# Fewer key chunks, a turned-query chunk for four heads, and the attention's first scores placed before the last value chunk

## The reference

```
proj = h @ w_in;  qa, ka, va, c_q, c_kv, k_r = split(proj)
q = (rmsnorm(c_q) @ w_uq).reshape(b, s, 8, 64 + 32)
q_nope, q_rope = q[..., :64], rope(q[..., 64:], cos, sin)
kv = (rmsnorm(c_kv) @ w_ukv).reshape(b, s, 8, 64 + 64)
k_nope, v = kv[..., :64], kv[..., 64:];  k_rope = rope(k_r, cos, sin)
sc = (q_nope . k_nope + q_rope . k_rope) * (64 + 32) ** -0.5
p = softmax(sc);  o = p @ v
```

## Time and profile before

| | |
|---|---|
| median of 3 runs | 1660.78 us (1659.16 to 1661.2) |
| profiled execution, its own time | 1662.77 us |
| its span, first to last instruction | 1660.7 us |
| mean granted TensorE clock | 0.996 |
| PE, DVE, ACT busy | 1620.9, 1235.5, 888.2 us |
| weight stream read | 282.68 MB at 171 GB/s over the span |

### The profile page before, as it was taken

One profiled execution on the slowest core, in us unless ns is written; L12 is line 12 of the kernel. 1 busy time (PEld: TensorE's weight loads), 2 busy tenths in 40 slices (PEclk: granted clock), 3 DMA queues, 4 the chain that ended last, 5 costly groups with the idle time before them and its releaser, 6 DMA issues.

```text
span 1660.7 us, 28594 instructions
## 1 busy us (share of the span) xinstructions
PE 1620.9 (98%) x10584; PEld 1468.4 (88%) x10584; DVE 1235.5 (74%) x1841; ACT 888.2 (53%) x1154; POOL 42.8 (3%) x55
## 2 busy tenths in 40 slices
PE   9989999999999999999999999999999999999998
PEld 8878999978899999878999999877999997899997
DVE  5765887778787787875887777447687787878787
ACT  5475545464764556565645464544554556665453
POOL 0001000000000000000000014000000000000000
PEclk9999999999999999999999999999999999999999
DMA  7253554544365544431554545543555454255543
GB/s 284 95 180 115 204 197 171 189 165 177 130 226 188 191 177 178 152 127 52 187 199 170 190 160 207 203 152 108 189 196 201 163 191 178 107 173 185 194 177 126
DMA packets 42113, 284.65 MB, mean 171 GB/s; under 512 B 4960, under 2 KB 5088, under 8 KB 9152
## 3 DMA queue, kind: packets, MB, share of 16 engines
q1 hardware_dynamic: 39840, 274.43, 45.2%
q0 software_dynamic: 2208, 9.32, 1.6%
HBM read 282.68 MB, written 1.05 MB: 171 GB/s over the span
## 4 chain that ended last, share of the span: by engine, by line
PE 84%; DVE 9%; issue 3%; ACT 3%; DMA 1%; DVEq 0%; SPq 0%; POOL 0%; ACTq 0%
PE bank L1774 14%; PE bank L1776 14%; PE bank L1775 14%; PE bank L1868 8%; PE bank L1869 8%; PE bank L1870 8%; PE bank L1820 4%; PE bank L1821 4%; PE bank L1822 4%; DVE w_lo L992 2%; DVE arena L1271 1%; ACT w_hi L554 1%; PE bank L1756 1%; PE bank L1917 1%; PE bank L2170 1%
## 5 line engine op out<-in xcount | busy, mean ns | idle before, releaser
L1774 PE MATMUL bank<-h_hi,w_hi 128*128 128x256 f32 (+1 forms) x2240 | 642.7, 287 | 9.8 <-DVE w_lo L992 6.3
L1775 PE MATMUL bank<-h_hi,w_lo 128*128 128x256 f32 (+1 forms) x2240 | 636.7, 284 | 0.0
L1776 PE MATMUL bank<-h_lo,w_hi 128*128 128x256 f32 (+1 forms) x2240 | 636.7, 284 | 0.0
L1774 PEld LDWEIGHTS bank<-h_hi,w_hi 128*128 128x128 f32 x2240 | 429.9, 192 | 18.2 <-issue 9.5
L1775 PEld LDWEIGHTS bank<-h_hi,w_lo 128*128 128x128 f32 x2240 | 430.0, 192 | 4.5 <-issue 1.4
L1776 PEld LDWEIGHTS bank<-h_lo,w_hi 128*128 128x128 f32 x2240 | 429.9, 192 | 0.9
L992 DVE TENSOR_TENSOR w_lo<-raw,w_hi 128x2048 fp32r<-128x2048 f32 (+3 forms) x115 | 244.9, 2132 | 115.2 <-ACT w_hi L554 114.9
L1298 DVE TENSOR_TENSOR w_lo<-raw,w_hi 128x2048 fp32r<-128x2048 f32 x145 | 327.6, 2285 | 1.6 <-ACT w_hi L753 1.6
L741 ACT ACTIVATE arena<-arena,par 128x256 f32<-128x256 f32 x220 | 120.5, 595 | 357.9 <-DVE arena L1257 354.6
L753 ACT ACTIVATE w_hi<-raw 128x2048 fp32r<-128x2048 f32 x150 | 286.1, 1907 | 19.8 <-PE bank L1870 19.7
L554 ACT ACTIVATE w_hi<-raw 128x2048 fp32r<-128x2048 f32 (+2 forms) x110 | 194.3, 1772 | 106.9 <-PE bank L1870 39.0
(11 more groups left out here) (196 smaller groups left out, 1294.2 us busy)
## 6 DMA issues: line engine op xcount, KB each, us to landing
raw<-wstream SPq DMA_DIRECT2D x254, 1024.0 KB, 4.8
arena<-window_bias POOLq DMA_DIRECT2D x4, 768.0 KB, 7.9
raw<-wstream SPq DMA_DIRECT2D x8, 256.0 KB, 3.1
arena<-dilated_bias POOLq DMA_DIRECT2D x8, 256.0 KB, 3.4
arena<-conv_rows POOLq DMA_DIRECT2D x2, 1024.0 KB, 4.8
raw<-wstream SPq DMA_DIRECT2D x4, 384.0 KB, 3.5
cst<-consts SPq DMA_DIRECT2D x1, 1088.0 KB, 11.7
x<-x_in SPq DMA_DIRECT2D x2, 512.0 KB, 5.1
```

What stands on the lines that cost most here:

```text
L1774: nc.tensor.matmul(dst, w_parts[0], x_parts[0], start=start, stop=False, **kw)
L1775: nc.tensor.matmul(dst, w_parts[1], x_parts[0], start=False, stop=False, **kw)
L1776: return nc.tensor.matmul(dst, w_parts[0], x_parts[1], start=False, stop=stop, **kw)
```

## The change

The rotated 32 columns of four heads now share a tile, and their swapped halves another, so that chunks 9 and 10 are all of the turned parts, 11 and 12 the plain parts of four heads each. Keys of two heads share a tile, and a chunk has four heads: two key chunks (13, 14) in place of four, since the unused value columns are no longer in them. The value chunks become 15 and 16, w_o 17 to 20. DVE's products with the tables cover 128 partitions of 256, for four heads at once, and its sums are one for each head, 32 partitions of 256; the tables are laid out four times down the partitions. ACT copies plain queries and keys head by head, four copies of 64 x 256 for each chunk.

PE computes the scores of heads 0 and 1 after the key chunks, before the value chunks (in nat before the last two), once the banks are free. The values go to banks outside the ring of three (`value_banks`). The wait for their copies moves to the first product with the values, and ACT makes the copies after the exponentials of heads 0 and 1 and before the first transposed copy.

There are four slots for bias tables instead of two; the two new ones lie in lat, free once the latents are normalized. In the mixer, ACT's split of chunk 5 moves ahead of the first reciprocal root. In nat, the split of chunk 13 moves from ahead of the attention into it, in halves (ACT at heads 2 and 3, DVE at 4 and 5), and ACT's halves of chunk 14 from heads 3 and 5 to 5 and 6.

```diff
-        return [CH] * 9 + [2 * 3 * P] * 4 + [2 * 2 * P] * 4 + [2 * 256] * 2 + [CH] * 4
+        return [CH] * 9 + [2 * 3 * P] * 4 + [2 * 2 * P] * 2 + [2 * 256] * 2 + [CH] * 4
...
+        def value_banks(name, c):
+
+            return (bank[4], bank[5]) if name == "mix" or c == 8 else (bank[6], bank[7])
...
+        def bias_slot(h):
+
+            return bias_a[:, h % 4, :] if h % 4 < 2 else flat(lat[:, 2 * (h % 4) - 4:2 * (h % 4) - 2, :])
...
-                        if h >= 2:
-                            pool.wait_ge(biased, bias_count(h - 2))
-                        pool.dma_start(bias_a[:, h % 2, :], bias_in[:, h * 512:(h + 1) * 512]).then_inc(bias_full[h % 2], 16)
+                        if h == 2:
+                            pool.wait_ge(hlo_done, DT + 5)
+                        if h >= 4:
+                            pool.wait_ge(biased, bias_count(h - 4))
+                        pool.dma_start(bias_slot(h), bias_in[:, h * 512:(h + 1) * 512]).then_inc(bias_full[h % 4], 16)
...
+                    if n == 1:
+                        last_values()
...
-                        if c:
+                        if c not in (0, 3):
...
+                            split_hi(c0 + 5)
                             inv_sqrt()
...
-                    for c in range(9, 19):
-                        if c < 17:
-                            split_hi(c0 + c + 2)
-                        src = bank[(c0 + c) % 3]
-                        if c < 17:
-                            dst = q_b if c < 13 else k_b
-                            j = (c - 9) % 4
-                            evac(c0 + c, dst[0:64, 2 * j:2 * j + 2, :], halves(src[0:64, :]), 1.0 if c < 13 else SCALE_B)
-                        elif c == 18:
-                            value_evac(c0 + 17, v_b, scaled=False, heads=0)
+                    for c in range(9, 15):
+                        split_hi(c0 + c + 2)
+                        if c >= 11:
+                            dst, src = (q_b, k_b)[c // 13], bank[(c0 + c) % 3]
+                            act.wait_ge(chunk_used, c0 + c + 1)
+                            for i in range(4):
+                                h = 4 * ((c - 11) % 2) + i
+                                ins = nc.scalar.activation(dst[0:64, h, :], src[64 * (i % 2):64 * (i % 2) + 64, (i // 2) * S:(i // 2 + 1) * S],
+                                                           ACT.Copy, scale=(1.0, SCALE_B)[c // 13])
+                            ins.then_inc(evac_done, 1)
+                            k["evac"] += 1
...
+                        2: lambda: half_hi_of(c0 + 17, 0), 3: lambda: half_hi_of(c0 + 17, 1),
+                        5: lambda: half_hi_of(c0 + 18, 0), 6: lambda: half_hi_of(c0 + 18, 1),
+                        9: lambda: half_hi_of(c0 + 19, 0), 10: lambda: half_hi_of(c0 + 19, 1),
                         11: lambda: y_squares(slice(0, 512), 0, 1),
-                        15: lambda: y_squares(slice(512, 768), 2, 2)}, dve_copies=(9, 11, 13, 15))
+                        15: lambda: y_squares(slice(512, 768), 2, 2)}, dve_copies=(9, 11, 13, 15),
+                        last_values=lambda: value_evac(c0 + 15, v_b, scaled=False, heads=0, banks=value_banks("mix", 15)))
...
-                        if c:
+                        if 0 < c < 11:
                             split_hi(c0 + c + 2)
                         if c < 8:
                             evac(c0 + c, pair(qk_n, c), bank[(c0 + c) % 3][:, :])
                             squares([(pair(qk_n, c), 512, evac_done, k["evac"])])
                         if 1 <= c <= 8:
                             inv_sqrt(512)
-                        if c >= 8 and c % 2:
-                            value_evac(c0 + c - 1, v_n, heads=4 * (c - 9))
-                    attention((0, 1, 2), None, {3: lambda: half_hi_of(c0 + 14, 0), 5: lambda: half_hi_of(c0 + 14, 1)})
+                        if c == 9:
+                            value_evac(c0 + 8, v_n, heads=0, banks=value_banks(name, 8))
+                    attention((0, 1, 2), None, {2: lambda: half_hi_of(c0 + 13, 0), 3: lambda: half_hi_of(c0 + 13, 1),
+                                                5: lambda: half_hi_of(c0 + 14, 0), 6: lambda: half_hi_of(c0 + 14, 1)},
+                              last_values=lambda: value_evac(c0 + 10, v_n, heads=8, banks=value_banks(name, 10)))
...
+                    def turned_products(i):
+
+                        src = bank[(c0 + 9 + i) % 3]
+                        dve.wait_ge(chunk_used, c0 + 9 + i + 1)
+                        dve.wait_ge(rope_step, 3)
+                        for n, table in enumerate((cos, sin)):
+                            nc.vector.tensor_tensor(rope_t[:, n, i * S:(i + 1) * S], src[:, n * S:(n + 1) * S], table, ALU.mult)\
                                      .then_inc(rope_step, 1)
...
+
+                    def turned_sums(i):
+                        dve.wait_ge(rope_step, 5 + 2 * i)
+                        for g in range(4):
+                            part = slice(32 * g, 32 * g + 32)
+                            nc.vector.tensor_tensor(q_b[64:96, 4 * i + g, :], rope_t[part, 0, i * S:(i + 1) * S],
+                                                    rope_t[part, 1, i * S:(i + 1) * S], ALU.add).then_inc(rope_step, 1)
+
+                    split_lo(c0 + 11)
+                    turned_products(0)
+                    split_lo(c0 + 12)
+                    turned_products(1)
+                    split_lo(c0 + 13)
+                    turned_sums(0)
+                    split_lo(c0 + 14)
+                    turned_sums(1)
+                    split_lo(c0 + 15)
+                    split_lo(c0 + 16)
...
+                              (0, 1, 2), None, {4: lambda: half_lo_of(c0 + 13, 0), 5: lambda: half_lo_of(c0 + 13, 1),
+                                                7: lambda: half_lo_of(c0 + 14, 0), 8: lambda: half_lo_of(c0 + 14, 1)})
...
+            def score_pair(scores, g):
+
+                g0 = k["heads"]
+                for e in (g, g + 1):
+                    if e >= 2:
+                        pe.wait_ge(*((biased, bias_count(e - 2)) if has_bias(e - 2) else (exp_done, e - 1)))
+                for j in range(2):
+                    for e in (g, g + 1):
+                        q, key = scores(e - g0, j)
+                        ins = nc.tensor.matmul(bank[e % 2][:, j * S:(j + 1) * S], q, key, start=True, stop=True)
+                        if j:
+                            ins.then_inc(score_done, 1)
...
+                    if g == g0:
+                        pe.wait_ge(evac_done, k["evac"])
...
-                score(g0)
...
+                    for c in range(9, 15):
+                        if c == 9:
+                            free = evac_v, v0 + 7
+                        elif c < 12:
+                            free = evac_done, e0 + c - 9
+                        elif c < 14:
+                            free = rope_step, (5, 7)[c - 12]
+                        else:
+                            free = evac_done, e0 + 3
+                        if c < 13:
+                            feature_chunk(c0 + c, 8, 3, 2, k["hlo"] if c == 9 else None, free)
+                        else:
+                            feature_chunk(c0 + c, 11, 2, 2, k["hlo"] + 3 if c == 13 else None, free)
+                    pe.wait_ge(evac_done, e0 + 5)
+                    score_pair(mix_scores, k["heads"])
+                    for c in (15, 16):
+                        token_chunk(c0 + c, c == 16, 11, 1, banks=value_banks(name, 15))
+                    k["hlo"] += 5
+                    k["ev"] += 7
+                    k["evac"] += 8
...
+                            if c == 10:
+                                pe.wait_ge(evac_done, e0 + 8)
+                                pe.wait_ge(nq_done, 5)
+                                score_pair(nat_scores, k["heads"])
+                                pe.wait_ge(stat_read, k["stat"])
+                            token_chunk(c0 + c, c % 2, banks=value_banks(name, c - c % 2))
...
+            for c in range(2):
+                turned = [np.concatenate([(NOPE + ROPE) * h + NOPE + part for h in range(4 * c, 4 * c + 4)])
+                          for part in (np.arange(ROPE), swap)]
+                tiles(a["w_uq"][0], *turned)
+            for w, width, n_chunks in ((a["w_uq"][0], NOPE + ROPE, 2), (a["w_ukv"][0], P, 2)):
+                pairs = [np.concatenate([span(width * h, NOPE), span(width * (h + 1), NOPE)]) for h in range(0, HB, 2)]
+                for c in range(n_chunks):
+                    tiles(w, pairs[2 * c], pairs[2 * c + 1])
```

More of the change, by code:

```diff
@@ L247, in build_program @@
         raw_full = [sem(f"raw_full{i}") for i in range(RING)]
-        bias_full = [sem(f"bias_full{i}") for i in range(2)]
+        bias_full = [sem(f"bias_full{i}") for i in range(4)]
         tables_loaded = sem("tables_loaded")
@@ L602, in evac, with value_evac @@
                 k["evac"] += 1
```

(39 more changed lines are left out.)

68 lines of the change are left out of this document (15 added, 53 removed).

## The result

The changed kernel takes 1652.45 us (median of 5 runs, 1650.83 to 1653.51) against 1661.2 before (5 runs, 1659.16 to 1663.38): ratio 0.9942, interval 0.9931 to 0.9954, faster by 8.75 us where 13.3 was forecast. The ratios given here are not quotients of the two medians (that would be 0.9947); by this ratio the gain is 9.6 us. The profiled execution is 1650.89 us long, its span 1648.9. Timed again beside the experiments, as e13, the kernel took 1651.16 us against 1663.28, ratio 0.9931 [0.9919, 0.9943], which is 11.5 us.

What follows compares the result with a forecast made beforehand. PE, busy 98% of the span, was taken as the bound, with mixer stalls on DVE, weight slots and bias tables. Mixer 10.9 plus nat 2.4 made 13.3 us off the median 1660.78: 1647.5, range 1642.5 to 1653.

Steps and rivals of the forecast that it cites:

- early product: Mixer: PE's scores of heads 0 and 1, made before the values, start near 81.6 after idling 0.4 us.
- add of heads 6 and 7: Mixer: DVE's bias add for the fourth pair starts at 96.1 instead of 106.99.
- wrong ones: Signs against: dilated_bias landings over 6 us, early PE idle over 1, clock under 1.00 at 82-100, nat's lead gone.
- Mixer: Mixer, up to the fourth pair's bias add: 10.9 us off, the 0.5 lost at the start included.
- Evacuation: Mixer: ACT's four 64x256 copies take 1.2 to 1.7 us a chunk in place of one 0.59 us copy; 1.2 taken.
- Split of chunk 5: Mixer start: ACT's split ahead of the reciprocal root delays the normalizing; 0.47 us stays, cost taken as 0.5.
- rotation: Mixer: DVE's twelve rotation instructions fall from 8.3 us to 5.0, at 0.42 each; bounds 4.2 and 8.3.
- Four tables: Mixer attention: bias tables requested early enough that the stall goes; one exposed landing would leave 7.4 us of gain.
- the largest stall: Mixer attention: with two bias tables, each new one lands 3.47 us after request; 15.1 us pass for four pairs.
- Rival B: Mixer gives less: tables share the queue with weight loads, one 3.5 us landing exposed, or copies cost 1.7; 1651.0, chance 0.15.
- Nat: Neighbourhood attention: earlier first product and moved splits bring the add of heads 8 and 9 forward 2.4 us; bounds 0, 5.4.
- rival A: Nat gives nothing: moved splits, or a granted clock that still falls, eat its lead; 1649.9, chance 0.15.

Runs made afterwards that it cites:

- e13: The changed kernel itself, unedited, timed again beside the experiments: 1651.16 us against 1663.28 before, ratio 0.9931.
- e6: Changed kernel with the split of the mixer's chunk 5 put back behind the reciprocal root: 1650.38 us, ratio 0.9928.
- e3: Kernel before with four bias table slots instead of two and nothing else: 1660.92 us, ratio 0.9992.
- e11: Changed kernel with two table slots and 18 idle transposes on PE ahead of the third pair's product: 1655.16 us, ratio 0.9958.
- e12: Kernel before with the mixer's repacking and moved chunk 5 split; two table slots, first scores after the values, nat as before: 1654.71 us, ratio 0.9962.
- e4: Changed kernel with two bias table slots instead of four: 1662.08 us, ratio 0.9985; five of 12 runs at 1654.2 to 1656.7, seven at 1661.9 to 1663.8.
- e9: Kernel before with nat's part of the change alone: 1662.43 us, ratio 0.9999.
- e1: Changed kernel with nat put back as before, leaving the mixer's part alone: 1652.87 us, ratio 0.9939.
- e7: Changed kernel with nat's chunk 13 split whole where DVE idles, chunk 14's ACT halves back at heads 3 and 5: 1647.6 us, ratio 0.9907.
- e8: Changed kernel with more idle PE transposes at conv0's entry, 36 instead of 24 and 6 between the halves: 1649.67 us, ratio 0.9922.
- e5: Changed kernel with the mixer's first scores after the value copies again: 1655.31 us, ratio 0.9959.

## Why the prediction was right, and where its size was off

**What came out.** The forecast was 1647.5 us with a range from 1642.5 to 1653; 1652.45 is inside by 0.55 us and 5 us from the value. Nearly every sign that was named as right came true in the trace: no DVE wait on dilated_bias, 24 fewer matmuls, the early product near 81.6, the add of heads 6 and 7 near 96, no stretch at 0.50 in nat. Only the add of heads 8 and 9 stands at 727.18 for 725.6, later by what conv0 lost. None of the wrong ones did (PE idled 0.86 us, the clock was 1.00 between 82 and 100), and still the time was short of the forecast: a lead laid out against one trace can be there in the next trace and be missing in the times.

**Mixer, right to 0.5 us.** 10.40 of 10.9. The positions in the text must be read from the mark, since this trace began 0.56 us earlier: the early product came 0.4 us later than laid out (81.42 for 81.6), the first value product 0.4 (88.23 for 88.4), the add of heads 6 and 7 0.5 (96.03 for 96.1). *Evacuation* was priced low: four 64x256 copies take 1.55 us, not 1.2, near the upper bound, and PE idles 0.86 us, not 0.4. The estimate from the Trainium skill ("ScalarE: Activation LUTs", What ACT_TABLE_LOAD costs), 1.32, lay between. *Split of chunk 5* cost 0.3, not 0.47 (e6). The *rotation* was read rightly: a 32x256 sum takes 0.44 us and a 128x256 product 0.38, where 0.42 was taken for each.

**Four tables, rightly sized in the sum, wrongly ranked.** The text called the table's wait "the largest stall"; alone its removal gives 1.8 us (e3), between repacking and early scores 1.5, and last of all 3.7 (e11 against the changed kernel). The bulk, 6.3, is the repacking (e12). But the slots are what keeps the early scores safe: without them the kernel takes as long as before in most runs (e4). Rival B had the tables share a queue with the weights; the page lists them as POOLq beside SPq. They did land later, 4.7 us for 3.4, within the slack.

**Nat, the step that failed.** The add of heads 8 and 9 came 2.33 us earlier, almost as laid out (2.4). But the term was priced against an execution whose clock had fallen for 7 us; the prediction saw the row of 0.50, and took its doubled pair as the kernel's own cost. In three other traces of the old order the fall is shorter and the order takes 28.6 to 28.8. What the term is worth is 0.3 to 0.5 us in traces and nothing in times (e9, e1): rival A's size, 2.0 us less. Of the two causes that A named, the clock is not the one, since it no longer falls. The moved splits are: made whole in DVE's idle stretch instead (e7), the same new order takes 25.03, 3.6 to 3.8 less than the old one. The Trainium skill ("TensorE: Matmul & The Clock Gate", What's actually happening) says that activity releases the throttle; e8 and e11, where idle transposes in a gap keep the clock at 1.00, agree.

**Conv0, not in the prediction.** 1.57 us are lost to a fall at a place that the change doesn't touch (e8 gives back 1.5). It stands in all five traces with the whole mixer change and conv0 unfilled (changed, e1, e6, e7, e13) and in one of seven others (e4; not in before, e3, e5, e9, e11, e12), though PE's two waits are 1.71 or 1.72 and 0.96 us in all twelve. Why the new mixer brings it, 240 us later, is open.

**The sum.** By the stretches 10.4 + 0.4 - 1.6 = 9.2 us, against 8.75 measured by the medians and 9.6 by the ratio. That they agree so well is partly luck, because e13, the same kernel, gained 11.5. The runs spread more than was thought: the kernel before took 1659.12 to 1665.35 in 23 runs beside e1, 0.4% and not the 0.1% that its first three runs suggested. The profiled executions alone differ by 11.88: that of before is 1.57 us above its median, with its long fall in nat, and that of the changed kernel 1.56 below its own, partly for its early start (e13's begins 1.53 us later and takes 1.65 more, with the same time from the mark to the end, 1617.6). Of the 4.5 us that are missing to 13.3, the traces give about 2.0 to nat, 1.6 to conv0 and 0.5 to the mixer; by e13 only 1.8 us are missing, so these shares hold for the traces, and how the times divide is not shown.

## What to carry to other kernels

Before a profiled microsecond is counted as won, look whether the granted clock was 1.00 around it: a fall can hit one execution of a kernel and spare the next (e4's two groups), so what it costs may belong to that execution and not to the order of work. A resource that isn't worth much alone (here two more table slots, 1.8 us) can be what makes another step safe, so try each edit of a change with and without the others. Before work is split into halves, look for a stretch in which its engine stands idle; e7 won 3.2 us in the trace by putting a whole split into one.

## What the runs showed of the hardware

In e4's profiled execution a PE gap of 2.22 us in an attention otherwise at 1.00 was followed by 20 us at the 1.2 GHz level. Seven of its twelve runs, this one among them, are some 7 us longer than the other five; with 2.1 us of idle transposes in the gap none of six was. In nat PE waits of 0.78 and 1.65 us were followed by 3 to 7 us of lower clock in four traces of four, while in the mixer's attention waits of 0.69 and 1.47 us were in one (e12) and not in three others (before, e3, e9). At conv0's entry waits of 1.71 and 0.96 us were followed by 3 us of lower clock in six traces of twelve. A bias table of 256 KB landed 3.0 to 3.5 us after issue in the attention of the kernel before, and 3.9 to 5.4 in that of the changed kernel, where SP requested 1 MB weight loads from 81.06 on; in the former it requested none between 89.66 and 106.
